# Expert results added to the residual rows by accumulating scatters

## The reference, cut to what matters

```python
h = x + hybrid_mixer(rms_norm(x, attn_norm), ...)
h = h + hier_moe(rms_norm(h, ffn_norm), ...)      # for each token: two experts of 32
return rms_norm(h, final_norm)
# an expert on a block of tokens:
hb = silu(xb @ w_gate[e]) * (xb @ w_up[e])        # 1024 -> 512
yb = hb @ w_down[e]                               # 512 -> 1024
# y[token] = the sum over its two experts of weight * yb
```

## Time and profile before

| | us |
|---|---|
| median of 3 runs | 1514.96 (1513.44 to 1522.62) |
| profiled execution, its time | 1514.61 |
| profiled execution, its span | 1513.0 |
| TensorE busy | 1406.0 (93%) |
| VectorE busy | 686.3 (45%) |
| ScalarE busy | 464.5 (31%) |
| GpSimd busy | 248.1 (16%) |
| moved by DMA | 402.20 MB, mean 266 GB/s |

### The profile page before, as it was taken

The page is one execution under the profiler, slowest core; times in us unless marked ns, Lnnn a source line. Parts: engine busy times, 40 slices in busy tenths (PEclk is TensorE's granted clock), DMA queues, the critical chain, the costliest instruction groups (busy, mean ns, idle before and its releaser), DMA issues.

```text
span 1513.0 us, 37631 instructions
## 1 busy us (share of the span) xinstructions
PE 1406.0 (93%) x15114; PEld 851.7 (56%) x15114; DVE 686.3 (45%) x1951; ACT 464.5 (31%) x1315; POOL 248.1 (16%) x319
## 2 busy tenths in 40 slices
PE   7999999999999999999997838999999999999984
PEld 4565665665656656656656525555555555555541
DVE  1574773864846747738648672111211122111206
ACT  2741832824626418328245100101110010100102
POOL 0000100001001001000010012344334333443320
PEclk9999999999999999999997758999999999999997
DMA  9954745646556447456453056999999999999867
GB/s 369 401 183 165 260 148 184 208 153 212 173 187 224 153 162 260 151 183 208 153 194 141 1 213 265 418 403 410 392 406 404 395 394 392 389 398 390 357 231 305
DMA packets 57390, 402.20 MB, mean 266 GB/s; under 512 B 10376, under 2 KB 10568, under 8 KB 35440
## 3 DMA queue, kind: packets, MB, share of 16 engines
q1 hardware_dynamic: 42224, 363.72, 63.6%
q0 software_dynamic: 15104, 37.80, 6.7%
HBM read 380.87 MB, written 29.36 MB: 271 GB/s over the span
## 4 chain that ended last, share of the span: by engine, by line
PE 79%; DVE 11%; ACT 4%; issue 3%; DMA 2%; POOL 0%; DVEq 0%; SPq 0%; POOLq 0%; ACTq 0%
PE ps L550 24%; PE ps L779 22%; PE ps L800 11%; DVE big L1112 6%; PE duo L705 4%; PE ps L705 3%; PE ps L486 2%; PE ps L662 1%; DMA big<-in_w_in 1%; PE duo L766 1%; PE duo L512 1%; PE duo L504 1%; ACT xin L925 1%; PE ps L728 1%; PE duo L790 1%
## 5 line engine op out<-in xcount | busy, mean ns | idle before, releaser
L779 PE MATMUL ps<-big 128*32 128x256 f32 x6144 | 339.7, 381 | 2.1 <-DVE big L1112 2.1
L779 PEld LDWEIGHTS ps<-big 128*32 128x32 f32 x6144 | 197.5, 110 | 134.5 <-issue 7.2
L550 PE MATMUL ps<-big,xin 128*128 128x386 f32 (+1 forms) x672 | 271.9, 541 | 0.2 <-DMA big<-in_w_in 0.2
L550 PE MATMUL ps<-big 128*128 128x512 f32 (+2 forms) x608 | 210.5, 498 | 11.3 <-DMA big<-in_w_in 11.3
L1112 DVE TENSOR_TENSOR big<-big 128x256 f32<-128x256 f32 (+5 forms) x294 | 157.6, 559 | 58.4 <-ACT big L891 35.5
L550 PEld LDWEIGHTS ps<-big,xin 128*128 128x128 f32 x672 | 123.0, 195 | 90.5 <-issue 50.4
L800 PE MATMUL ps<-big 128*32 128x256 f32 x3072 | 172.4, 380 | 0.9 <-ACT big L1068 0.9
L1546 DVE SCALAR_TENSOR_TENSOR big<-big,ps 128x128 f32<-128x128 f32 x96 | 27.1, 282 | 321.9 <-ACT big L1064 321.9
L550 PEld LDWEIGHTS ps<-big 128*128 128x128 f32 x608 | 113.2, 192 | 88.7 <-issue 70.6
L800 PEld LDWEIGHTS ps<-big 128*32 128x32 f32 x3072 | 97.3, 110 | 66.1 <-issue 5.0
L1064 ACT ACTIVATE big<-ps 128x128 f32<-128x128 f32 x96 | 26.7, 278 | 335.9 <-PE ps L779 335.9
(11 more groups left out here) (255 smaller groups left out, 1537.7 us busy)
## 6 DMA issues: line engine op xcount, KB each, us to landing
big<-in_w_gu SPq DMA_DIRECT2D x64, 2048.0 KB, 10.0
big<-in_w_in SPq DMA_DIRECT2D x64, 1024.0 KB, 4.8
big<-in_w_down SPq DMA_DIRECT2D x32, 2048.0 KB, 10.2
big<-in_w_in SPq DMA_DIRECT2D x64, 772.0 KB, 4.7
big<-in_w_in SPq DMA_DIRECT2D x32, 512.0 KB, 4.4
hn_rows<-big POOLq DMA_DIRECT2D x8, 1024.0 KB, 6.9
big<-y_rows SPq DMA_DIRECT2D x8, 1024.0 KB, 11.8
big<-in_x SPq DMA_DIRECT2D x8, 512.0 KB, 8.7
```

The lines of the kernel that those rows point to most:

```text
L550: last = t_.matmul(ps[6 + n % 2][:, 0:w], x_src[:, k, :], wv[:, k % KH, :], start=k == 0, stop=k == KD - 1)
L779: last = t_.matmul(ps[GU[t]][TG * j:TG * (j + 1), 0:2 * HC], xT[:, k, TG * t:TG * (t + 1)], wgu[par][k // KH][:, :, k % KH, HC * j:HC * (j ...
```

## The change: what it does

The scatters go to `h_rows` and carry an add: each 1 KB quarter row is added to what lies in memory at its destination. `y_rows` is gone. `hn_rows` has one row per token, so both of a token's slots read the same row, and one table of indices (token times 4 plus quarter) serves gather and scatter. The load of the residual rows ahead of the end is gone; the closing stretch loads eight tiles of 512 KB from `h_rows` into `cm_h`, ScalarE squares each into `cm_sq`, and VectorE scales each in place, in groups of three, three and two. TensorE has no part in it.

```diff
-        cm_y = [part(2 * DM) for _ in range(NT)]
+        cm_h = [part(DM) for _ in range(NT)]
+        cm_sq = [part(DM) for _ in range(NT)]
...
-            sp.wait_ge(sem("hn_stored"), 32 * NT)
-            sp.dma_start(cm_h, h_d.rearrange("(t p) d -> p t d", p=P)).then_inc(sem("ch_loaded"), 16)
-            sp.dma_start(fgain, a["final_norm"].partition_broadcast(P)).then_inc(sem("ch_loaded"), 16)
+            sp.dma_start(fgain, a["final_norm"].partition_broadcast(P)).then_inc(sem("gain_loaded"), 16)
             sp.wait_ge(sem("y_added"), 1)
             for t in range(NT):
-                sp.dma_start(cm_y[t], y_v[t]).then_inc(sem(f"loaded{t}" if t < 4 else f"y_loaded{t - 4}"), 16)
+                sp.dma_start(cm_h[t], h_v[t]).then_inc(sem(f"loaded{t}" if t < 4 else f"h_loaded{t - 4}"), 16)
             for t in range(NT):
                 sp.wait_ge(sem("c_out"), t + 1)
-                sp.dma_start(out_v[t], cm_y[t][:, 0:DM]).then_inc(sem("out_stored"), 16)
+                sp.dma_start(out_v[t], cm_h[t]).then_inc(sem("out_stored"), 16)
...
-            for n, t in enumerate(PE_TILES):
-                for c in range(2):
-                    t_.matmul(ps[2 * n + c][:, :], ident, cm_h[:, t, 512 * c:512 * c + 512], start=True, stop=False)
-            for n, t in enumerate(PE_TILES):
-                wait_y(pe, t)
-                for c in range(2):
-                    for k in range(2):
-                        o = DM * k + 512 * c
-                        last = t_.matmul(ps[2 * n + c][:, :], ident, cm_y[t][:, o:o + 512], start=False, stop=k == 1)
-                    last.then_inc(sem("p_sum"), 1)
...
             for t in range(NT):
-                if t in PE_TILES:
...
+                wait_h(act, t)
+                s.activation(cm_sq[t], cm_h[t], ACT.Square, accum_out=ssx[:, t:t + 1]).then_inc(sem("c_sq"), 1)
...
-            seq(v.tensor_scalar(tokf[:, 0:NT], cn("c128"), cn("pcol"), 2.0 * CT, ALU.add, ALU.mult))
-            v.tensor_scalar(tokf[:, NT:], tokf[:, 0:NT], 2.0 * CT, None, ALU.add)
+            seq(v.tensor_scalar(tokf[:, 0:NT], cn("c128"), cn("pcol"), float(CT), ALU.add, ALU.mult))
+            v.tensor_scalar(tokf[:, NT:], tokf[:, 0:NT], float(CT), None, ALU.add)
...
-                cseq(tt(mx[:, some], ssx[:, some], tx_[:, some], ALU.add))
-                cseq(v.tensor_scalar(mx[:, some], mx[:, some], 1.0 / DM, EPS, ALU.mult, ALU.add))
-                rsqrt(mx[:, some], rx[:, some], ssx[:, some], cseq)
+                cseq(v.tensor_scalar(mx[:, some], ssx[:, some], 1.0 / DM, EPS, ALU.mult, ALU.add))
+                rsqrt(mx[:, some], rx[:, some], tx_[:, some], cseq)
                 for o in range(t, t + n):
...
+                    v.scalar_tensor_tensor(cm_h[o], cm_h[o], rx[:, o:o + 1], fgain, ALU.mult, ALU.mult) \
+                        .then_inc(sem("c_out"), 1)
...
-            summed(0)
-            summed(2)
-            normed(0, 3)
-            summed(4)
-            summed(6)
-            normed(3, 4)
-            normed(7, 1)
+            normed(0, 3)
+            normed(3, 3)
+            normed(6, 2)
...
-                pool.dma_start(hn_v[i], heads(hnb, 2)).then_inc(sem("hn_stored"), 16)
+                pool.dma_start(hn_v[i], hnb).then_inc(sem("hn_stored"), 16)
...
-                    g.indirect_dma_start(y_q, bass.IndirectOffsetOnAxis(ap=ydst[par][:, t:t + 1], axis=0),
-                                         yo[par][:, t * YC:(t + 1) * YC], None, bounds_check=2 * CT * SEQ - 1,
-                                         oob_is_err=False).then_inc(sem(f"y_sent{par}"), 16)
+                    g.indirect_dma_start(h_q, bass.IndirectOffsetOnAxis(ap=ydst[par][:, t:t + 1], axis=0),
+                                         yo[par][:, t * YC:(t + 1) * YC], None, bounds_check=CT * SEQ - 1,
+                                         oob_is_err=False, compute_op=ALU.add).then_inc(sem(f"y_sent{par}"), 16)
```

More of the change, by code:

```diff
@@ L49 @@
 N_OVER = NB_MAX - NE
-PE_TILES = (1, 3, 5, 7)
 X_LOADS = ((1, 2), (3, 4), (5, 6, 7))
@@ L163, in heads, with build @@
     return ap.unsqueeze(1).to_broadcast([ap.shape[0], n, ap.shape[1]])
-def build(nc, a, out, hn_d, h_d, y_d):
+def build(nc, a, out, hn_d, h_d):
     ctx = ExitStack()
@@ L289, in build @@
         used[0] = 0
-        cm_y = [part(2 * DM) for _ in range(NT)]
+        cm_h = [part(DM) for _ in range(NT)]
+        cm_sq = [part(DM) for _ in range(NT)]
         assert used[0] <= 2 * 3 * 4096
         used[0] = moe_used
-        cm_h = three(part(NT * DM), NT, DM)
         fgain = part(DM)
@@ L319, in build @@
         x_view = a["x"][0].rearrange("(t p) d -> t p d", p=P)
-        hn_v = hn_d.rearrange("(t p k) d -> t p k d", p=P, k=2)
-        h_v = h_d[0:SEQ, :].rearrange("(t p) d -> t p d", p=P)
+        hn_v = hn_d.rearrange("(t p) d -> t p d", p=P)
+        h_v = h_d.rearrange("(t p) d -> t p d", p=P)
         hn_q = hn_d.rearrange("t (j d) -> (t j) d", j=CT)
-        y_q = y_d.rearrange("t (j d) -> (t j) d", j=CT)
-        y_v = y_d.rearrange("(t p k) d -> t p (k d)", p=P, k=2)
+        h_q = h_d.rearrange("t (j d) -> (t j) d", j=CT)
         out_v = out[0].rearrange("(t p) d -> t p d", p=P)
@@ L366, in build, with wait_h @@
         W_UNITS = 2 * NG * NT // 4
-        def wait_y(eng, t):
+        def wait_h(eng, t):
             if t < 4:
@@ L372, in wait_y @@
             else:
-                eng.wait_ge(sem(f"y_loaded{t - 4}"), 16)
+                eng.wait_ge(sem(f"h_loaded{t - 4}"), 16)
         DVE_LINKS, ACT_LINKS = 80, 2
@@ L832, in _ @@
             down(last_pair * 2 + 1, last_pair, 1)
-            pe.wait_ge(sem("y0_ready"), last_pair * 2 + 3)
-            pe.wait_ge(sem("y1_ready"), last_pair * 2 + 3)
-            pe.wait_ge(sem("ch_loaded"), 32)
-            for n, t in enumerate(PE_TILES):
-                for c in range(2):
-                    t_.matmul(ps[2 * n + c][:, :], ident, cm_h[:, t, 512 * c:512 * c + 512], start=True, stop=False)
-            for n, t in enumerate(PE_TILES):
-                wait_y(pe, t)
-                for c in range(2):
-                    for k in range(2):
-                        o = DM * k + 512 * c
-                        last = t_.matmul(ps[2 * n + c][:, :], ident, cm_y[t][:, o:o + 512], start=False, stop=k == 1)
-                    last.then_inc(sem("p_sum"), 1)
         @block.scalar
@@ L1573, in _ @@
             y_right(last_pair * 2 + 1, last_pair, 1)
-            dve.wait_ge(sem("ch_loaded"), 32)
+            dve.wait_ge(sem("gain_loaded"), 16)
             cc = [0]
@@ L1582, in cseq @@
                 dve.wait_ge(sem("comb_chain"), cc[0])
-            cseq(v.memset(tx_, 0.0))
             def normed(t, n):
@@ L1679, in gather @@
                                          bass.IndirectOffsetOnAxis(ap=idxs[par][:, t:t + 1], axis=0),
-                                         bounds_check=2 * CT * SEQ - 1, oob_is_err=False).then_inc(sem(f"tok_loaded{par}"), 16)
+                                         bounds_check=CT * SEQ - 1, oob_is_err=False).then_inc(sem(f"tok_loaded{par}"), 16)
             def add_rows(b, q, par):
@@ L1745 @@
     out = nc.dram_tensor("out_0", (1, SEQ, DM), F32, kind="ExternalOutput").ap()
-    hn_d = nc.dram_tensor("hn_rows", (2 * SEQ, DM), F32, kind="Internal").ap()
+    hn_d = nc.dram_tensor("hn_rows", (SEQ, DM), F32, kind="Internal").ap()
     h_d = nc.dram_tensor("h_rows", (SEQ, DM), F32, kind="Internal").ap()
-    y_d = nc.dram_tensor("y_rows", (2 * SEQ, DM), F32, kind="Internal").ap()
-    build(nc, aps, out, hn_d, h_d, y_d)
+    build(nc, aps, out, hn_d, h_d)
     r = _run(nc, [arrays], core_ids=[0])
```

## The result

| | before | changed |
|---|---|---|
| median, us | 1514.02 | 1578.53 |
| lowest to highest | 1512.86 to 1522.62 | 1567.87 to 1584.39 |
| profiled execution: time, span | 1514.61, 1513.0 | 1567.87, 1566.3 |

The changed kernel is slower: ratio 1.0412, 95% interval 1.038 to 1.0444. The likeliest case of the prediction, A, was wrong; its rival B, priced at 1560 us for the middle of its bounds, is what happened. The profiled execution is the lowest of six.

What follows compares the result with a forecast made beforehand. The prediction took TensorE to bound the expert loop, with a closing stretch of transfers and small steps behind it. Span 1513.0 - 15.1 (closing stretch) + 1.8 (last scatters) = 1499.7, plus 1.6 around it: 1501.3 us, range 1497 to 1587.

Steps and rivals of the forecast that it cites:

- A: Expert loop: the add is hidden, with landings 0 to 2.2 us longer; 1497 to 1506 us, chance 0.47.
- B: Expert loop: GpSimd's wait for a landing ahead of the gathers becomes the bound; 1560 us, chance 0.33 of over 1% slower.
- closing stretch: After the last scatter: half-size loads, squares on ScalarE and unbroken VectorE work end the span at 1497.9, 15.1 us gained.
- spare of 2.2 us a block: GpSimd in the loop: 4.4 us idle per pair with two landings in series, so each may grow by 2.2 us.
- formula: Loop loss once GpSimd's order is the bound: 30(d - 2.2) - 6 us, the 6 being late-gather spare used once.
- d: Growth of an adding scatter's landing: taken as 1.2 us, half an undisturbed trip of 2.3, with bounds 0 and 6.3.
- Issue: GpSimd's three scatter issues of 1.0 us a block: longer issue counts threefold in d; no growth was priced.
- Landing: Scatter's trip to memory: 1.2 us growth hidden in the loop, 1.8 us lost at the end where nothing covers it.
- Rival C: Expert loop: the DMA engines become the bound if an add costs several writes; 1571 us at six times, chance 0.10.

Runs made afterwards that it cites:

- e1: The changed kernel with the add left out of its scatters, so the expert sum is not formed: 1502.65 us, ratio 0.9916 to the kernel before.
- e8: The kernel before with a dummy GpSimd operation of 1.9 us ahead of each block's scatter, no add: 1519.62 us, ratio 1.0023.
- e9: The kernel before with two dummy GpSimd operations, 3.9 us together, ahead of each block's scatter, no add: 1560.59 us, ratio 1.0294.
- e4: The changed kernel with the odd block's gather issued ahead of the wait for the odd scatter's landing: 1536.76 us, ratio 1.0128 to the kernel before.
- e6: The changed kernel with 8 KB weight packets and the odd gather ahead of the wait for the odd landing: 1506.57 us, ratio 0.9943 to the kernel before.
- e10: The kernel before with three dummy GpSimd operations, 5.8 us together, ahead of each block's scatter, no add: 1590.11 us, ratio 1.0486.
- e2: The changed kernel, add kept, with each 2 MB weight load cut into four, giving 4 KB packets: 1515.96 us, ratio 1.0009 to the kernel before.

## Why the prediction was wrong

**The closing stretch was right.** Forecast 15.1 us gained; measured 14.2 from first load to end. e1, which has it with an undisturbed loop, is at 1502.65, against the 1501.3 forecast for a hidden scatter and within A's own range of 1497 to 1506. VectorE ran unbroken from the third square on, as forecast; its chain began 8.4 us after the first load's issue where 7.4 was forecast.

**The structure of the loop was right.** Two landings a pair in series on GpSimd, a spare of 2.2 us a block, late gathers as the way to TensorE: e8 (1.9 us, hidden) and e9 (3.9 us; 37.5 us lost in the loop where the formula has 45) stand on both sides of that threshold, and e4 and e6 give time back by order. The formula's slope was too steep, as e10 shows.

**The step that failed is the size of d**, "I take half an undisturbed trip, d = 1.2". With it the loop was to hide the scatter; measured, d was 5.3 on average, above the spare of 2.2. The prediction had named this as what would make it wrong, "a landing more than 2.2 us longer in the loop". Two terms were mis-sized:

- *Issue.* It was said to count threefold, and then taken as zero. It grew from 1.00 to 1.57 us, so 1.7 of the 2.2 us were gone before the landing was counted.
- *Landing.* The rows of an undisturbed trip were the nearest by name, but not by state. Undisturbed, the adding scatter was hardly slower: the last two land 2.7 and 3.4 us after their issue began, where 2.3 stood for the last one before, and 0.6 of that is the longer issue. Under load the wait grew by 3.6 us on average and by 10 at worst, since the packets shrank from 4 KB to 1 KB and each took a turn behind a 16 KB packet. That the price of this transfer depends on its number of packets times its neighbours' size was missing from the working.

The sum, d = 1.7 + 3.6 = 5.3 on average, lies within the prediction's bounds of 0 and 6.3, and by its formula gives 30 x 3.1 - 6 = 87 us in the loop. Measured 64. That the 1560 us of B came out near was in part luck: its d of 4.3 was too small, and its slope too steep. The formula lacks that landings shorten when TensorE waits, because its weight loads pause. In the changed kernel the SP queue issued nothing from 1149.1 to 1167.6 us, and the even scatter of 1156.06 had its last row in memory 1.8 us after its last issue. The odd one of 1169.45, with 9 weight packets passing for each engine, landed after 7.6 us, while that of 1207.38, with the loads back in step, took 18.7. The line of the one at 1169.45:

```profile
1182.44 0.19 POOL L1626 COPY idx<-big 128x3 int32 x1 [7.60 <-DMA h_rows<-big,ydst]
```

**Rival C** was close to nothing in the changed kernel (350 GB/s, no wait of TensorE for weights in the loop). The queue's share for a byte did grow: GpSimd's queue took 13.6% of the DMA engines' time for 10.90 MB from 1000 to 1400 us, against 8.1% for 12.08 MB. The DMA ceiling is near, as e2 shows, where 4 KB weight packets and adds together made TensorE wait for weights.

```profile
q0 software_dynamic: 12136, 10.90, 13.6%
```

**The rule of the Trainium skill** (Collectives: The Full Stack, "The bandwidth ceiling"), that an add costs its second read, gives an estimate of 0.32 us of an engine for a 4 KB result, twice the measured 0.16. The packet records have four packets of 0.10, so 0.40. The rule, which was measured on another path, was a little short in time and says nothing on what decided here, the number of turns.

**Left open.** Why the issue on GpSimd takes longer was not looked into, nor why a plain scatter's landing follows the turns only in part. The changed kernel's spread of 16 us over six runs is wider than before, which a loop that alternates between short and long landings would give, but no run separates it.

## What to carry to other kernels

Cost a transfer by its packets as well as its bytes, and price each packet with the largest packet that another queue puts beside it; here the small packets beside 16 KB loads paid in latency before they paid in bandwidth. Where an engine issues, waits for the landing and issues again, work out its spare per turn, and put work that does not need the landing ahead of the wait. A delay of known length in the unchanged kernel measures that spare cheaply.

## What the runs showed of the hardware that was not expected

- An indirect scatter that adds moves each 1 KB row as a packet of its own (0.10 us), where the same scatter without the add moves 4 KB packets (0.16 us); its issue on GpSimd takes 1.57 us for 128 rows, not 1.00.
- Each slot of such a scatter stands as a packet of its own, the empty ones with 8 bytes (8192 of 1 KB and 4096 of 8 bytes), and in the longest waits 23 to 25 weight packets for each engine passed beside the 24 slots of a block.
- With no loads beside it the adding scatter lands only 0.4 to 1.1 us later than the plain one. Beside 16 KB packets a block takes up to 18.7 us beyond its last issue.
- A GpSimd subtract in place on 128x1024 takes 1.89 us, while one product on 128x256 in the mixer takes 1.06 (L1632 of before) and another 0.71 (L1630), so the first was no basis to estimate from.
